# Two experts with fixed places, finer interleaving and an earlier output gate in a one-core model kernel

## What is computed

```python
p_top_g, g_idx = lax.top_k(p_group, 1)
p_top_e, e_idx = lax.top_k(jax.nn.softmax(e_logits, axis=-1), TOP_K)      # 2 of 8
for gi in range(N_GROUPS):
    hid = silu(t @ w_gate[gi]) * (t @ w_up[gi]) * combine[:, gi]
    out = out + hid @ w_down[gi]
...
x = x + gt2 * hier_moe(modulate(rms_norm(x, norm2_g), sh2, sc2), ...)
# second block, per half (context first, then latent tokens)
q, k, v, gates = mlstm_inputs(h @ w_in, ...)      # convolution on q and k
h = mlstm_chunkwise(q, k, v, ...)                 # 4 heads, chunks of 128, both directions
y_m = head_rmsnorm(h * sigmoid(u_o)) * silu(u_z)
y_p = multiscale_pool(u_pool) * silu(u_pg)
y = concat(y_m, y_p) @ w_out
```

## Time and profile before

| | |
|---|---|
| median of 3 runs | 1671.16 us (1663.08 to 1674.93) |
| the profiled execution | 1670.68 us |
| its span, first to last instruction | 1668.8 us |
| mean granted TensorE clock | 0.962 of 2.4 GHz |
| TensorE busy | 1529.8 us (92%) |
| DMA | 397.59 MB, mean 238 GB/s |
| router stage | 434 to 475 us |
| expert stage, to the end of its last pass | 477.6 to 1088.1 us |

### The profile page before, as it was taken

How to read it: one execution, slowest core, us unless ns; L and a number is a source line. 1 busy time by engine, 2 the same in 40 slices (tenths; PEclk the granted TensorE clock), 3 DMA queues, 4 the chain that set the end, 5 groups by cost and what they waited for, 6 DMA issues and landing times.

```text
span 1668.8 us, 21989 instructions
## 1 busy us (share of the span) xinstructions
PE 1529.8 (92%) x9293; PEld 1047.2 (63%) x9293; DVE 487.9 (29%) x1233; ACT 336.2 (20%) x690; POOL 4.1 (0%) x8
## 2 busy tenths in 40 slices
PE   6999999999799889978989998969889999999897
PEld 3655689888774334634456644548666675888665
DVE  2200086423342311223113000028342232022471
ACT  2311151211212102021200000023212222021461
POOL 0000000000000000000000000000000000000000
PEclk9999999999799799999999999989899999999998
DMA  9989642131269889999999999942122313423100
GB/s 375 408 349 371 237 154 78 51 131 75 104 273 421 344 359 415 391 418 419 419 402 414 406 403 422 368 174 89 64 98 105 151 51 151 152 69 145 51 1 26
DMA packets 54304, 397.59 MB, mean 238 GB/s; under 512 B 6359, under 2 KB 13688, under 8 KB 16440
## 3 DMA queue, kind: packets, MB, share of 16 engines
q1 hardware_dynamic: 40384, 341.85, 51.0%
q10 hardware_dynamic: 13240, 52.16, 7.9%
q0 software_dynamic: 576, 2.10, 0.4%
HBM read 389.80 MB, written 6.29 MB: 237 GB/s over the span
## 4 chain that ended last, share of the span: by engine, by line
PE 80%; DMA 9%; DVE 4%; ACT 3%; issue 2%; SPq 1%; ACTq 1%; DVEq 0%; POOL 0%; POOLq 0%; PEldq 0%; PEld 0%
PE bank L692 16%; PE bank L1435 13%; PE bank L1450 9%; PE bank L2366 7%; DMA work<-in_moe_w_up 4%; PE bank L2383 4%; PE bank L1555 3%; PE bank L1550 3%; PE bank L526 3%; PE bank L2352 2%; PE bank L723 2%; PE bank L1146 2%; PE bank L1160 2%; DMA work<-in_ab_pool_w 1%; DMA work<-in_moe_w_gate 1%
## 5 line engine op out<-in xcount | busy, mean ns | idle before, releaser
L692 PE MATMUL bank<-H,ring 128*128 128x256 f32 (+1 forms) x960 | 245.2, 412 | 1.0 <-ACTq L297 0.7
L692 PEld LDWEIGHTS bank<-H,ring 128*128 128x128 f32 x960 | 181.4, 191 | 52.8 <-issue 28.8
L2366 PE MATMUL bank<-ring,work 128*32 128x512 f32 (+1 forms) x768 | 137.6, 630 | 15.8 <-DMA ring<-in_moe_w_up 5.7
L1435 PE MATMUL bank<-H,work 128*128 128x256 f32 x512 | 115.8, 385 | 0.4 <-issue 0.4
L1435 PE MATMUL bank<-H,ring 128*128 128x256 f32 x512 | 113.4, 381 | 0.0
L1435 PEld LDWEIGHTS bank<-H,work 128*128 128x128 f32 x512 | 97.1, 192 | 19.6 <-issue 6.5
L1435 PEld LDWEIGHTS bank<-H,ring 128*128 128x128 f32 x512 | 97.9, 192 | 13.6
L2366 PEld LDWEIGHTS bank<-ring,work 128*32 128x32 f32 (+1 forms) x768 | 36.3, 122 | 103.9 <-issue 84.8
L1450 PE MATMUL bank<-work,H 128*128 128x512 f32 x192 | 85.2, 596 | 0.0
L1450 PE MATMUL bank<-ring,H 128*128 128x512 f32 x192 | 83.4, 593 | 0.0
L2383 PE MATMUL bank<-ring,work 128*32 128x512 f32 (+1 forms) x384 | 68.0, 624 | 4.1 <-issue 2.2
(11 more groups left out here) (426 smaller groups left out, 1937.9 us busy)
## 6 DMA issues: line engine op xcount, KB each, us to landing
ring<-in_moe_w_gate SPq DMA_DIRECT2D x48, 1024.0 KB, 10.6
ring<-in_moe_w_up SPq DMA_DIRECT2D x48, 1024.0 KB, 9.0
ring<-in_moe_w_down SPq DMA_DIRECT2D x48, 1024.0 KB, 12.1
work<-in_ab_w_in ACTq DMA_DIRECT2D x28, 1024.0 KB, 10.0
ring<-in_ab_w_in SPq DMA_DIRECT2D x14, 2048.0 KB, 7.6
work<-in_ada_w SPq DMA_DIRECT2D x12, 2048.0 KB, 14.9
ring<-in_w_in SPq DMA_DIRECT2D x12, 2048.0 KB, 10.2
work<-in_w_mod SPq DMA_DIRECT2D x12, 2048.0 KB, 9.4
```

The lines of the kernel that those rows point to most:

```text
L692: mm = nc.tensor.matmul(tile_bank(i)[:, 0:n], weight(c, k, j * P, (j + 1) * P), rhs(k), start=(k == 0), stop=(k == kt - 1))
L1435: mm = nc.tensor.matmul(b[:, j * T:(j + 1) * T], w_k(m, n, k, at, at + P), H[:, k, m.s], start=(k == 0), stop=(k == DT - 1), skip_group_ch ...
L2366: mm = nc.tensor.matmul(bank[b][rows, :], gath[:, k, rows], half_slot[(load_at[n + half] + e) % NHALF][:, (k % 4) * 512:(k % 4 + 1) * 512] ...
```

## The change

Four things are changed, all in the router and expert stages:

1. Experts 0 and 1 always take the first two wide places: a large number is added to their key in the ranking, so the other six wide places go to the fullest of the rest. They form the first pass. Then come the six passes of four and three passes of two. The gate and up halves of the two (eight loads, `fixed_sync`) are issued by SP ahead of the router, as soon as the ring slots are released by the stages before. The test for `over` takes the fixed experts in.
2. The tokens of this first pass are gathered in the router (`gather_pe` into banks 6 and 7, with a `pick` made from the fixed experts' places alone). The context's Q[0], which ran there, moves to the head of the body, which has 116 turns now.
3. The turns are taken at thirteen points a pass instead of nine: also in the middle of each step. How many is a table for each pass (`TURNS`, 5, 18, 20, 16, 21, 15, 12, 2, 2 and 2 turns); the four turns ahead of the first pass are gone.
4. The context's output gate O is woven into the recurrence: after each four turns of `mlstm_pe` one quarter of O (`row_halves_pe`, 128 tokens by 256 columns) is computed, and its sigmoid kept in `o_rows`; the product with the heads is made behind the recurrence (`o_late_dve`). In pooling, the four means run during PU[1] and the mixing after them.

```diff
+N_FIXED = 2
+PASSES = [(0, N_FIXED)] + [(N_WIDE + 4 * i, 4) for i in range((NX - N_WIDE) // 4)] + [(2 * i, 2) for i in range(N_FIXED // 2, N_WIDE // 2)]
+    key_no = np.arange(NX) - FIXED_KEY * np.maximum(N_FIXED - np.arange(NX), 0)
...
+        def row_halves_pe(pe, m, n):
+            w_wait(pe, m, n)
+            for t in range(TT):
+                for half in range(2):
+                    b = a_turn(pe)
+                    at = m.s.start + t * P
+                    for k in range(DT):
+                        mm = nc.tensor.matmul(b[:, 0:MD], H[:, k, at:at + P], w_k(m, n, k, half * MD, (half + 1) * MD), start=(k == 0), stop=(k == DT - 1))
+                    mm.then_inc(a_mm, 1)
+                    if t + half == 2:
+                        w_done(m, n)
+                    yield
...
         def router_pe(pe):
-            head = head_pe(pe)
...
+            pe.wait_ge(pick_ready, 1)
+            gather_pe(FIRST_GATHER)
...
+        def fixed_sync(sp):
+            at = 0
+            for n in range(FIXED_STEPS):
+                w, half = (wg, wu)[n // 2], n % 2
+                for i in range(N_FIXED):
+                    displaced = before_moe[at // 2] if at < 2 * RING else early_last[0]
+                    if at % 2 == 0 and displaced is not None:
+                        sp.wait_ge(*last_use[displaced])
+                    sp.dma_start(half_slot[at], half_src(w, i, half)).then_inc(step_in[n], 16)
+                    at += 1
...
-        FILL_FOUR, FILL_TWO = (2, 2, 2, 2, 2, 2, 2, 1, 1), (0, 0, 0, 1, 0, 1, 0, 0, 0)
+        TURNS = ((0, 1, 0, 1, 0, 0, 0, 1, 1, 0, 1, 0, 0),
+                 (1, 1, 1, 1, 1, 0, 1, 1, 2, 2, 3, 2, 2),
+                 (2, 2, 3, 2, 2, 2, 0, 1, 1, 2, 1, 1, 1),
+                 (1, 1, 1, 1, 1, 0, 1, 1, 1, 1, 2, 2, 3),
+                 (2, 2, 2, 2, 2, 2, 2, 2, 1, 1, 0, 2, 1),
+                 (1, 1, 1, 1, 1, 0, 1, 2, 2, 2, 1, 1, 1),
+                 (1, 1, 1, 1, 1, 0, 1, 1, 1, 1, 1, 1, 1),
+                 (0, 0, 0, 0, 0, 0, 0, 1, 0, 0, 1, 0, 0),
+                 (0, 0, 0, 0, 0, 0, 0, 1, 0, 0, 1, 0, 0),
+                 (0, 0, 0, 0, 0, 0, 0, 1, 0, 0, 1, 0, 0))
...
             def project(p, b, n, at):
-                    mm.then_inc(step_used, 1)
-                    if at + half < 3:
-                        fill(body, p, at + half)
+                        if k % 4 == 3:
+                            mm.then_inc(step_used, 1)
+                        if k % 2 == 1 and at + k // 2 < 7:
+                            fill(body, p, at + k // 2)
...
-                yield from mlstm_pe(pe, m, 2 * hp)
-                yield from mlstm_pe(pe, m, 2 * hp + 1)
-                yield from rows_pe(pe, m, O[hp])
+                yield from weave(both(mlstm_pe(pe, m, 2 * hp), mlstm_pe(pe, m, 2 * hp + 1)), row_halves_pe(pe, m, O[hp]), 4, 1)
```

More of the change, by code:

```diff
@@ L1260, in weave, with both @@
                         yield
+        def both(a, b):
+            yield from a
+            yield from b
         def norm_sum_turn(pe, s):
@@ L1332, in __init__ @@
                 self.ss, self.dn = ar.take(4), ar.take(2, 1)
+                self.o_rows = None if wide else ar.take(TT, 2 * MD)
                 flat = self.kw.rearrange("p d t n -> p (d t n)")
@@ L1935, in pool_late_dve @@
             a_seen(NPOOL)
-            for _ in range(8):
+            for _ in range(4):
                 yield
@@ L2024, in build @@
         over = ar.take(1).bitcast(I32)
+        m_dense = ar.mark()
+        gath = ar.take(DT, P)
+        pick = ar.take(TT, P)
         m_moe = ar.mark()
@@ L2079, in router_pe @@
             mm.then_inc(lane_mm, 1)
-            next(head)
             pe.wait_ge(lane_out, 4)
@@ L2087, in router_pe @@
             mm.then_inc(lane_mm, 1)
-            for _ in head:
-                pass
         def router_act(act, chain):
@@ L2104, in router_act @@
             nc.scalar.activation(r3, r3, ACT.Exp).then_inc(rt_e, 1)
-            head = head_act(act)
-            for _ in head:
-                pass
+            gate_in_act(act, mixers[0])
+            take_low_act(act, 0, FIRST_GATHER)
         def router_dve(dve, chain):
@@ L2191, in build @@
         NHALF = 8
-        gath = ar.take(DT, P)
-        pick = ar.take(TT, P)
         spot = ar.take(TT, NX)
@@ L2224, in half_src @@
         def half_src(w, e, half):
+            if isinstance(e, int):
+                return w[e, :, half * HALF:(half + 1) * HALF]
             return w[bass.ds(e, 1), :, half * HALF:(half + 1) * HALF].rearrange("e p n -> p (e n)")
+        FIXED_STEPS = NHALF // N_FIXED
+        def fixed_sync(sp):
[8 more added lines that the diff above has]
+                    at += 1
         def sparse_sync(sp):
             for p, (first, experts) in enumerate(PASSES):
-                e = [sp.value_load(ids[0:1, first + i:first + i + 1], min_val=0, max_val=NX - 1) for i in range(experts)]
+                e = list(range(N_FIXED)) if p == 0 else [sp.value_load(ids[0:1, first + i:first + i + 1], min_val=0, max_val=NX - 1) for i in range(experts)]
                 for j, w in enumerate((wg, wu, wd)):
@@ L2240, in build, with fill @@
         step_of = [n for n in range(6 * NPASS) for _ in range(PASSES[n // 6][1])]
-        FILL_FOUR, FILL_TWO = (2, 2, 2, 2, 2, 2, 2, 1, 1), (0, 0, 0, 1, 0, 1, 0, 0, 0)
-        def fill(body, p, i):
-            for _ in range((FILL_FOUR if PASSES[p][1] == 4 else FILL_TWO)[i]):
-                next(body, None)
-        def start(body):
-            for _ in range(4):
+        TURNS = ((0, 1, 0, 1, 0, 0, 0, 1, 1, 0, 1, 0, 0),
[9 rows of a table added]
+        assert len(TURNS) == NPASS
+        def fill(body, p, *slots):
+            for _ in range(sum(TURNS[p][i] for i in slots)):
                 next(body, None)
@@ L2349, in gather @@
                     pe.wait_ge(py_out, 2 * p - 2)
-                for k in range(DT):
-                    for t in range(TT):
-                        mm = nc.tensor.matmul(bank[2 + k // 4][:, (k % 4) * P:(k % 4 + 1) * P], hrows[:, t, k * P:(k + 1) * P], pick[:, t, :],
-                                              start=(t == 0), stop=(t == 1), skip_group_check=True)
-                    if k % 4 == 3:
-                        mm.then_inc(gath_mm, 1)
+                gather_pe(GATHER)
             def project(p, b, n, at):
@@ L2384, in down @@
                                                       start=(f == 0), stop=(f == 3), skip_group_check=True)
-                    mm.then_inc(step_used, 1)
-                    fill(body, p, 5 + half)
-            gather(0)
-            start(body)
+                        if f % 2 == 1:
+                            mm.then_inc(step_used, 1)
+                        fill(body, p, 9 + f)
             for p in range(NPASS):
@@ L2881, in step_on @@
                 next(body, None)
-        def both(a, b):
-            yield from a
-            yield from b
         def mix_pe(pe):
```

199 lines of the change are left out of this document (102 added, 97 removed).

## The result

| | before | after |
|---|---|---|
| median | 1673.05 us (4 runs, 1663.08 to 1679.83) | 1694.2 us (4 runs, 1690.96 to 1701.28) |
| ratio | | 1.0137, 95% interval 1.0076 to 1.0198 |
| expert stage, first to last pass | 477.6 to 1088.1 us | 464.2 to 1111.1 us |

The change costs 1.4%, some 21 us; I had forecast 1662, and the time is outside my range. The stage starts 13.4 us earlier and ends 23.0 us later, so its ten passes take 646.9 us for 610.5. What follows the last pass is 2.6 us shorter (578.1 us to the end of the span, for 580.6). So the whole loss, and more, is in the ten passes.

A forecast was written before the change was run, and what follows sets the result against it. TensorE and the transfers were both taken as almost full, each pass going by the scarcer. Passes end at 1056.9 + 18.0 - 4.0 + 9.0 = 1079.9 against 1088.1, 8.2 us less: 1662 us, range 1640 to 1688.

The forecast's parts named there:

- the ledger: Ten expert passes, each the larger of TensorE's and the transfers' time: 592.5 us before, 589.9 after.
- allowance of 9 us for new losses: Expert passes: 6 us for early arrival at pass 1's steps, 3 us where passes 5 and 6 meet; bounds 0 and 25.
- Rival C: Passes of four: turns inside steps hold back slot releases, the queue runs dry, 31 us lost, about 1692 us; chance 0.16.
- Start and moved work: Expert stage: pass 0 starts at 467 and takes 43.5 us; TensorE's work up to the last pass's end grows by 12.0 us.
- Early loads: Ahead of the router: eight loads, 20 us of transfers, move into a nearly idle stretch.
- Rival B: First pass: early loads are worth nothing, transfers idle there and later waits return, 1671 us; chance 0.14.
- Row numbers: VectorE in the recurrence: their 4.0 us wait goes, as they now fall into pass 0.
- Pooling: Expert product behind three means on VectorE: a stall of some 7 us stays as before.
- The weave of O: Output gate in the recurrence: an O quarter costs what half a row tile did, adding nothing to TensorE.
- The tail: After the last pass: unchanged, about 20 us until ScalarE sums the rows, the body's last three turns under that.
- The rule on loops that wait: TensorE's clock: a loop that makes it wait for DMA runs cold, so removed waits pay twice.
- rival A: Expert passes: finer turn points remove most waits, 21.2 us less, 1649.5 us; chance 0.28.

The follow-up runs named there:

- even: Changed kernel with 17 turns in each pass of four, only behind the steps (2, 3, 2, 4, 2, 4): 1664.4 us, ratio 0.9962.
- counts: Changed kernel with its own turns per pass, but placed as in even, none inside a step: 1667.2 us, ratio 1.0002.
- even_inside: even with its counts kept nearly the same between releases, but part of the turns put inside the steps: 1691.5 us, ratio 1.0145.
- outer: Changed kernel with the same turns per pass, every turn inside a step moved behind that step: 1694.5 us, ratio 1.0135.
- even_late: even with the two fixed experts' loads held back until the routing's expert numbers are there: 1664.6 us, ratio 0.9990.
- tail_p0: even_tail with two turns in the first pass instead of five, the three moved behind step 5 of passes 1, 2 and 4: 1658.9 us.
- dealt_tail: even_tail with turns dealt by TensorE time (17, 18, 16, 20, 17, 11), behind the steps, six left for the tail: 1668.6 us.
- even_o_behind: even with the output gate computed as rows behind the recurrence again: 1674.7 us, ratio 1.0013.
- even_tail: even with 14 turns in pass 6 instead of 17, six left for the summing of the rows: 1655.2 us, ratio 0.9941.

## Why the prediction was wrong

- **The step that failed** is the ledger, "each pass as the larger of TensorE's time and the transfers'", with its allowance of 9 us for new losses (bounds 0 and 25). It lets a pass balance its own account, as if every load could wait for its turn. The ring holds two steps, so balance is needed over each stretch from a release to the step that needs what it let in. In the passes of four of after these stretches were 7 to 38 us long, and TensorE came to 26 of the 36 steps in under the 20 us that eight half loads take (even: 17, counts: 11). So the allowance for new losses, 9 us with a bound of 25, came to 43: pass 1 was put at 71.5 us and took 90.2, pass 6 at 76.3 and took 87.3, the ten at 589.9 plus 23 and took 646.9. Of the 30 us between after and even, about 19 go through the transfers and 11 stay with the loads halved; the other 13 of the 43 no run takes apart. The division over passes, on which I spent the working, is worth 3 us by medians (counts against even, with the 10.4 us wait in counts).
- **Rival C** had the number (1692) and the sign, and I gave it 0.16. Its mechanism, a turn inside a step that holds back four slots, was shown by even_inside (27 us) and, with the loads halved, by its absence (3 us). But it is not the sole cause here: outer took the inside turns away and kept the time, with the clumps left and a new wait of 9.4 us. Either alone reaches after's time, outer with the help of that wait. That C's number came out so close is luck in part: its sum, one point in four at 3.5 us, was a guess, the 35 points hold 49 turns, and it left out the clumps and the waits in the context's chain. The point from which I said it decides, a DMA share under 0.93, was met in three of the six passes; over all six it was 0.91.
- **Start and moved work** were right in kind: start 464.2 for 467, first pass 45.1 for 43.5. TensorE's busy time in the stage grew by 24.0 us by the windows, 12.0 of them the moved work. The rest stays open. The clock isn't shown to blame: (1 - clock) x length is 26.7 us in after, 26 in before; records may be missing.
- **Early loads.** Rival B had it: they are worth nothing that even_late can tell. I had counted them as relief in pass 0 and let their 20 us flow into the ledger. The first pass needs 12 loads in 43 us, and its ring is full either way; making it shorter only moved its turns (tail_p0).
- **Row numbers:** the 4 us stall went, as forecast.
- **Pooling:** the 7 us stall I kept "as before" was 0.6 us in after. In after three means do stand ahead of the expert product on VectorE, as I had said, and TensorE never waits for that product; in outer, counts and dealt_tail one to three means stand there too, and it waits 9.4 to 10.7 us. So the order on VectorE alone doesn't price it: it hangs on what TensorE has to do meanwhile.
- **The weave of O** was put at nothing; it may be worth 10 us with the even table (even against even_o_behind). It doesn't do so by filling the recurrence's waits on VectorE, which are the same without it (13.7 against 13.2 us); the traces put the difference into pass 2, and its cause stays open.
- **The tail** I called unchanged, with three turns under 20 us. I saw the room and did not price it: three turns more were worth 9 us by medians (even_tail), 0.2% or 4 us by the ratios.
- **The rule on loops that wait** (the Trainium skill, "TensorE: Matmul & The Clock Gate", section "Loop structure matters more than you think") I gave only to rival A, as a gain that would double. It works the other way as well: the rows of even_inside show 3.64 us for 1.92 right behind a wait, at a granted clock of 0.50 for 1.00, and the trace agrees with the rule.

One reading of the prediction was off without weight for the result: in the windows from 725 to 1018.7 us other than the first, TensorE was busy 91 to 99%, not 86 to 99.

Open: why even_inside loses 7 us more of "moving" time than the others; and what dealing by time would give without the pooling wait, which was not tried.

## What to carry to other kernels

With a ring of a few slots, ask of a schedule two numbers at every step, not one at every pass: the time between two releases (if it is longer than the ring can fill, the transfers stand) and the time from a release to the step that needs the load (if it is shorter than the transfers queued, the consumer stands). Filler work belongs behind the step that releases, in portions as equal as its own chain allows, and not where all slots are held (27 us here with whole loads, 3 with halves). Count the turns in measured time: a turn of a chunk took 3.5 us, one of the recurrence 1.3. Standing time of a queue alone is no cause; look which wait ends last at the consumer. And price a new division alone before its other parts: here the table turned a gain of 0.4% (even) into a loss of 1.4%.

## What the runs showed of the hardware

- The granted clock follows single waits: sixteen like matmuls took 3.4 to 3.6 us right behind the five waits of 4.2 to 7.7 us in even_inside (granted clock 0.50 to 0.56), 2.5 us behind one of 3.1 (0.73), and 1.9 us behind one of 1.8 (1.00).
- That makes such waits dearer than their length: inside turns added 15 us of waits on weights (35.2 against 20.4) and 20 us of busy time, and nearly all of both went when the loads were halved (2.4 us of waits, 1.2 of busy time).
- The six passes moved their bytes in 454 to 456 us in six kernels with times from 1664 to 1695 us (before, after, outer, counts, even, even_late): in these the rate did not suffer from the order of the turns. In even_inside the moving took 461.5 us.
